# A two-layer streaming encoder on one core: halves of two attention output units moved into the end of attention, and the engines' loops written out

## What is computed

```python
for l in range(DEPTH):                                   # 2 layers
    h = rmsnorm(x, attn_norm_g[l])
    proj = h @ w_in[l]
    q, k, v, conv_in, gate_logits = jnp.split(proj, SPLITS, axis=-1)
    q, k = apply_rope(q), apply_rope(k)
    y_attn = sliding_window_sink_attention(q, k, v, attn_sinks[l]) @ w_attn_o[l]
    ca, cb = jnp.split(conv_in, 2, axis=-1)
    u = causal_dwconv(ca * sigmoid(cb), conv_dw_w[l], conv_dw_b[l])      # width 31
    y_conv = silu(layernorm(u, conv_ln_g[l], conv_ln_b[l])) @ w_conv_o[l]
    g_attn, g_conv = jnp.split(gate_logits, 2, axis=-1)
    x = x + (sigmoid(g_attn) * y_attn + sigmoid(g_conv) * y_conv) @ w_out[l]
    up = causal_dwconv(rmsnorm(x, ffn_norm_g[l]) @ w_ffn_up[l], ffn_dw_w[l], ffn_dw_b[l])   # width 3
    gt, val = jnp.split(up, 2, axis=-1)
    x = x + (silu(gt) * val) @ w_ffn_down[l]
return rmsnorm(x, final_norm_g)
```

## Time and profile before

| what | value |
|---|---|
| median of 3 runs | 914.47 us (913.42 to 919.29) |
| the profiled execution | 913.93 us |
| its span, first to last instruction | 912.1 us |
| mean granted TensorE clock | 0.976 |
| PE busy | 854.9 us, 94% |
| DVE, ACT, POOL busy | 620.8, 479.2, 406.5 us |
| read from HBM | 142.31 MB |

### The profile page before, as it was taken

How to read it: one execution, slowest core, us unless ns; L and a number is a source line. 1 busy time by engine, 2 the same in 40 slices (tenths; PEclk the granted TensorE clock), 3 DMA queues, 4 the chain that set the end, 5 groups by cost and what they waited for, 6 DMA issues and landing times.

```text
span 912.1 us, 18341 instructions
## 1 busy us (share of the span) xinstructions
PE 854.9 (94%) x6764; PEld 825.9 (91%) x6764; DVE 620.8 (68%) x1182; ACT 479.2 (53%) x714; POOL 406.5 (45%) x94
## 2 busy tenths in 40 slices
PE   2799999899999999999979999998999999999996
PEld 2799988788999999999969998896899999999995
DVE  6586889925368876656537878993535787566563
ACT  4354357636455655555555334774744656456455
POOL 4577735464722242232257873554574122422423
PEclk8899999999999999999989999999999999999998
DMA  7355423324444555455425552332434445545551
GB/s 263 114 180 177 177 93 139 139 93 140 155 153 155 185 192 195 168 193 181 176 96 185 186 185 93 140 139 93 139 139 152 172 181 188 187 181 184 184 184 47
DMA packets 20512, 144.20 MB, mean 158 GB/s; under 512 B 2400, under 2 KB 2656, under 8 KB 3296
## 3 DMA queue, kind: packets, MB, share of 16 engines
q1 hardware_dynamic: 19872, 142.62, 43.7%
q10 hardware_dynamic: 576, 0.75, 0.2%
HBM read 142.31 MB, written 1.05 MB: 157 GB/s over the span
## 4 chain that ended last, share of the span: by engine, by line
PE 71%; DVE 13%; issue 8%; ACT 5%; DMA 1%; ACTq 0%; DVEq 0%
PE pu L716 19%; PE pu L718 18%; PE pu L717 18%; DVE pc L492 4%; ACT whi L226 2%; PE ps L716 2%; PE ps L718 2%; PE ps L717 2%; DVE wlo L618 1%; PE pc L718 1%; PE pt L717 1%; PE pt L716 1%; PE pt L718 1%; PE pc L716 1%; PE po L737 1%
## 5 line engine op out<-in xcount | busy, mean ns | idle before, releaser
L198 POOL TENSOR_TENSOR wlo<-raw,whi 128x2048 fp32r<-128x2048 f32 x88 | 405.8, 4613 | 497.4 <-ACT whi L226 497.4
L226 ACT ACTIVATE whi<-raw 128x2048 fp32r<-128x2048 f32 x134 | 254.7, 1902 | 25.6 <-PE pu L718 22.7
L716 PE MATMUL pu<-hh,whi 128*128 128x256 f32 x800 | 233.4, 292 | 23.5 <-ACT hh L243 21.7
L716 PE MATMUL pu<-uh,whi 128*128 128x256 f32 x832 | 237.2, 285 | 5.4 <-DVE ul L596 3.2
L717 PE MATMUL pu<-ul,whi 128*128 128x256 f32 x832 | 235.4, 283 | 0.0
L718 PE MATMUL pu<-uh,wlo 128*128 128x256 f32 x832 | 235.4, 283 | 0.0
L718 PE MATMUL pu<-hh,wlo 128*128 128x256 f32 x800 | 228.2, 285 | 0.0
L717 PE MATMUL pu<-hl,whi 128*128 128x256 f32 x800 | 228.2, 285 | 0.0
L492 DVE SCALAR_TENSOR_TENSOR pc<-upad,par,pc 128x256 f32<-128x256 f32 x464 | 187.1, 484 | 0.3
L716 PEld LDWEIGHTS pu<-hh,whi 128*128 128x128 f32 x800 | 155.4, 194 | 27.5 <-ACT hh L243 22.5
L716 PEld LDWEIGHTS pu<-uh,whi 128*128 128x128 f32 x832 | 159.6, 192 | 7.8 <-issue 7.5
(11 more groups left out here) (142 smaller groups left out, 1144.7 us busy)
## 6 DMA issues: line engine op xcount, KB each, us to landing
raw<-in_weights SPq DMA_DIRECT2D x134, 1024.0 KB, 4.8
x<-in_x_t SPq DMA_DIRECT2D x2, 512.0 KB, 5.5
out_y<-qk SPq DMA_DIRECT2D x2, 512.0 KB, 2.6
par_all<-in_params ACTq DMA_DIRECT2D x1, 472.0 KB, 10.2
const<-in_const ACTq DMA_DIRECT2D x1, 130.0 KB, 7.0
probs<-in_positions ACTq DMA_DIRECT2D x1, 128.0 KB, 4.6
gf<-in_final_g ACTq DMA_DIRECT2D x1, 4.0 KB, 12.3
```

The source lines that it names most:

```text
L198: nc.gpsimd.tensor_tensor(wlo[s][:, :], raw[s][:, :], whi[s][:, :].bitcast(f32), ALU.subtract).then_inc(lo_ready[s], 1)
L226: A(whi[s][:, :], raw[s][:, :], ACT.Copy).then_inc(hi_ready[s], 1)
L716: MM(out, whi[s][:, w], hi, start=start, stop=False, skip_group_check=accumulate)
```

## The change

PE's end of attention: for the first two attention output units, the products with the first four channel tiles of o (the heads of the first key head, groups 0 to 3, complete since long) are split off as `group_half(i, 0)`: 24 matmuls each. Unit 21's stands before the last transposes, unit 22's between `values(6)` and `values(7)`. All of the first three mean pairs move behind `values(7)`, and the second halves follow them. ACT forms the high part of unit 23 before, and no longer behind, the last evictions.

All `Fori` loops become Python loops, so the counts waited for are constants; `par` becomes a slice of `par_all`, the copy goes, and `par_ready` counts 5 a layer and not 6. The sums of squares at the start no longer mark `unit_done`, so every count waited for on it is one less (`finished`). The two units beyond the last layer, their loads and splits, go.

```diff
+        def finished(l, u):
+
+            return uses(l, u) + 1
...
-            with sp.Fori(1, DEPTH * USES) as r:
+            for r in range(1, DEPTH * USES):
                 for s in range(RING):
                     sp.wait_ge(lo_ready[s], r)
-                    load_unit(s, bass.ds(r * RING + s, 1))
-
-            for s in range(AHEAD):
-                sp.wait_ge(lo_ready[s], DEPTH * USES)
-                load_unit(s, slice(DEPTH * UNITS + s, DEPTH * UNITS + s + 1))
+                    load_unit(s, slice(r * RING + s, r * RING + s + 1))
+
...
-                act.wait_ge(unit_done[s], l * USES + n + 1)
+                if l * USES + n > 0:
+                    act.wait_ge(unit_done[s], l * USES + n)
...
-            with act.Fori(0, DEPTH) as l:
+            for l in range(DEPTH):
+                par = par_all[:, l * NPAR:(l + 1) * NPAR]
...
                     A(gate[:, :, i, :], pu[u % RING][:, :, :], ACT.Tanh, scale=0.5).then_inc(gate_ready, 1)
-                    if i < NT - 1:
-                        next_high(l, u)
+                    next_high(l, u)
                 evict_transposed(GROUPS - 1)
                 high_of_o(GROUPS - 2)
                 high_of_o(GROUPS - 1)
-                next_high(l, U_AO - 1)
                 next_high(l, U_AO)
                 next_high(l, U_AO + 1)
...
-                V.tensor_copy(par[:, :], par_all[:, bass.ds(l * NPAR, NPAR)]).then_inc(par_ready, 1)
-                dve.wait_ge(par_ready, l * 6 + 1)
+            for l in range(DEPTH):
+
+                par = par_all[:, l * NPAR:(l + 1) * NPAR]
...
-                with dve.Fori(0, FFN_STEPS // 2 - 1) as r:
+                for r in range(FFN_STEPS // 2 - 1):
...
+                def group_half(i, group):
+
+                    s, n = (U_AO + i) % RING, uses(l, U_AO + i)
+                    if group == 0:
+                        pe.wait_ge(*result_read(l, U_AO + i - RING))
+                        pe.wait_ge(hi_ready[s], n + 1)
+                        pe.wait_ge(lo_ready[s], n + 1)
+                        pe.wait_ge(oh_ready, l * GROUPS + N_CHUNKS)
+                        pe.wait_ge(ol_ready, l * GROUPS + N_CHUNKS)
+                    else:
+                        pe.wait_ge(oh_ready, l * GROUPS + GROUPS)
+                        pe.wait_ge(ol_ready, l * GROUPS + GROUPS)
+                    for m in range(2):
+                        for k in range(GROUP_PAIRS * group, GROUP_PAIRS * (group + 1)):
+                            last = product(pu[s][:, m, :], s, 2 * k + m, oh[:, k, :], ol[:, k, :],
+                                           k == 0 and m == 0, k == NT - 1, True)
+                    if group == 1:
+                        last.then_inc(unit_done[s], 1)
+
                 for i in range(GROUPS):
                     if i + 1 < GROUPS:
                         standard(U_GATE + i + 1, hh, hl)
                     else:
-                        mean_pair(0)
-                        mean_pair(1)
+                        group_half(0, 0)
                     transpose_probs(i)
                     if i:
                         values(i - 1)
                     if i + 2 < GROUPS:
                         scores(i + 2)
-                mean_pair(2)
+                group_half(1, 0)
                 values(GROUPS - 1)
...
-                for i in range(2):
-                    standard(U_AO + i, oh, ol, o_ready if i == 0 else None)
+                for p in range(3):
+                    mean_pair(p)
+                group_half(0, 1)
+                group_half(1, 1)
                 mean_pair(3)
                 standard(U_AO + 2, oh, ol)
```

More of the change, by code:

```diff
@@ L87, in hybrid_encoder @@
         par_all = sb("par_all", [P, DEPTH * NPAR])
-        par = sb("par", [P, NPAR])
         gf = sb("gf", [P, NT])
@@ L260, in _ @@
                     u = U_GLU + i
-                    act.wait_ge(unit_done[u % RING], uses(l, u) + 2)
+                    act.wait_ge(unit_done[u % RING], finished(l, u))
                     if i >= 2:
@@ L371, in hidden_tile @@
                     for half, col in ((0, gcol), (1, vcol)):
-                        A(fbuf[:, ab, half, :], up[:, ab, half, :], ACT.Identity, scale=par[:, bass.ds(col + 2, 1)],
-                          bias=par[:, bass.ds(col + 3, 1)]).then_inc(f_conv0, 1)
+                        A(fbuf[:, ab, half, :], up[:, ab, half, :], ACT.Identity, scale=par[:, col + 2:col + 2 + 1],
+                          bias=par[:, col + 3:col + 3 + 1]).then_inc(f_conv0, 1)
                     if split is not None:
@@ L405, in _ @@
                 ffn_step(FFN_STEPS - 1, 0, True)
-                for s in range(AHEAD):
-                    split_high(l, s, USES)
+                if l < DEPTH - 1:
+                    for s in range(AHEAD):
+                        split_high(l, s, USES)
                 for i in range(4):
@@ L656, in hidden_tile @@
                         acc = fbuf[:, ab, half, shift:T]
-                        last = V.scalar_tensor_tensor(acc, up[:, ab, half, 0:T - shift], par[:, bass.ds(col, 1)], acc,
+                        last = V.scalar_tensor_tensor(acc, up[:, ab, half, 0:T - shift], par[:, col:col + 1], acc,
                                                       ALU.mult, ALU.add).then_inc(f_tap, 1)
@@ L744, in _ @@
             for p in range(NT // 2):
-                last = sum_pair(po[:, 0, :], sq, p, sq_ready, p + 1)
-                if p < RING:
-                    last.then_inc(unit_done[p], 1)
+                sum_pair(po[:, 0, :], sq, p, sq_ready, p + 1)
             pe.wait_ge(c_in, 16)
             swap, ident = const[:, C_SWAP:C_SWAP + P], const[:, C_ID:C_ID + P]
-            with pe.Fori(0, DEPTH) as l:
+            for l in range(DEPTH):
                 def standard(u, hi, lo, ready=None, between=None):
@@ L890, in ffn_step @@
                     down_unit(1, k - 2, 1 - parity)
-                with pe.Fori(0, FFN_STEPS // 2) as r:
+                for r in range(FFN_STEPS // 2):
                     ffn_step(r * 2 + 1, 1)
@@ L926 @@
     layers = []
-    units = np.zeros((DEPTH * UNITS + AHEAD, P, UNIT), np.float32)
+    units = np.zeros((DEPTH * UNITS, P, UNIT), np.float32)
     for l in range(DEPTH):
```

41 lines of the change are left out of this document (19 added, 22 removed).

## The result

| | kernel before | changed kernel |
|---|---|---|
| median | 916.88 us (913.42 to 919.63, 4 runs) | 905.93 us (904.79 to 906.86, 4 runs) |
| the profiled execution | 913.93 us, span 912.1 | 904.79 us, span 903.0 |
| mean granted clock | 0.976 | 0.985 |

The ratio of the two is 0.9884, with a 95% interval of 0.9855 to 0.9913: the change makes the kernel faster by 0.9 to 1.5%. Forecast were 907.5 us as the median and 907.1 for a profiled execution; measured were 905.93 and 904.79. The kernel before was 914.47 us when the forecast was made, the median of three runs, and is 916.88 with the fourth: its runs lie near 914 and near 919. So between the medians it is 10.95 us, or 1.16%, and between the profiled executions 9.14.

A forecast was written before the change was run, and what follows sets the result against it. TensorE, busy 94% of the span, was taken as the bound, so only its standing time could be won. 3.9 + 0.65 + 1.32 + 0.9 = 6.8 us off 913.93 gave 907.1 profiled, 907.5 median; range 903.5 to 911.5.

The forecast's parts named there:

- 1. Attention's end: From values(6) to mean_pair(3): 12.76 us of work at full clock, 14.67 expected; gain 2.1 and 1.8, together 3.9 us.
- the early split on ACT: High part of unit 23 formed ahead of ACT's last eviction: costs nothing, bound 0 to 1.9 us.
- the clock: Behind values(6) at attention's end: 4.3 us at the lower level taken, a loss of 1.9 us.
- S cannot move: S, the start of values(6) at 181.18 in layer 0, stays because PE waits there for DVE's low part of group 5.
- 2. The heads of the layers: Written-out loops at layer starts: 0.65 us in layer 0 and 1.32 at the boundary.
- The boundary: Between layers, DVE's small steps run while ACT works on the root: gain 1.32 us, bounds 0 and 1.32.
- 3. The head of the feed-forward loop: Without register work, 0.29 and 0.15 us less on two passes: 0.44 a layer, 0.9 in all, bounds 0 and 2.3.
- 4. At nothing: Register operations elsewhere, SP's static addresses, loads and splits beyond the last layer, dropped unit_done marks: no gain.
- The clock stays up: Rival: no lower clock at attention's end, gain 10.7 us, time 903.8; chance 0.12.
- The clock takes most of it: Rival: clock low for 6.8 us at attention's end, tail gives 1.7, sum 4.6, time 909.9; chance 0.18.
- Instruction supply: Rival: written-out code stalls on instruction fetches of 5.05 us each; four give 927.7 us; chance 0.05.
- The written-out part gives nothing: Rival: boundary bound by ACT's root in another way, attention's end alone gives 3.9, time 910.5; chance 0.07.

The follow-up runs named there:

- after: The changed kernel itself, its first runs and profile, against the kernel before: median 905.93 us, ratio 0.9884.
- tail_only: The kernel before with all its hardware loops, only the end of attention reordered on PE and ACT: 908.29 us, ratio to before 0.9914.
- late_split: The changed kernel with ACT's high part of unit 23 behind the last evictions again: 905.16 us, ratio to before 0.9881.
- loops_only: The changed kernel with the old end of attention on PE and ACT, loops still written out: 915.22 us, ratio to before 0.9983.
- loops_again: loops_only unchanged, for a second profile: 913.76 us.
- second_hole: The changed kernel with two mean pairs ahead of the last transposes again, unit 21's first half after values(6), unit 22's after the third mean pair: 910.63 us.
- fill: The changed kernel with both first-group halves ahead of values(6) and the mean pairs spread into remaining waits: 899.59 us, ratio to before 0.9818.
- after_again: The changed kernel unchanged, run again beside tail_only and loops_only: 906.78 us, ratio to before 0.9897.
- fill_dve: fill_hw with VectorE's loops alone written out, its parameter copy kept: 899.47 us, ratio to before 0.9821.
- fill_hw: The order of fill with the kernel before's hardware loops on every engine: 902.02 us, ratio to before 0.9845.

## Why the prediction was right, and where its steps missed

**The time and the sign** came out: 905.93 against 907.5 forecast, inside the range. The profiled gain was 9.1 against 6.8, 2.3 more. Part of that closeness is luck. The end of attention gave 2.55 us more than forecast and the row of taps 1.26 where nothing was forecast; the heads of the feed-forward loop, the start and layer 0's first units gave 1.5 less. And the median of before moved by 2.4 us with one more run: counted from 916.88, the forecast gain of 7.0 would have read 909.9. The measured 1.16% is over the 1% to which the prediction gave a chance of 0.18, but the interval, 0.9 to 1.5%, reaches to both sides of it.

**1. Attention's end.** The count of work was right within 0.1: 12.76 us forecast at the full clock, 12.67 and 12.68 measured wherever the clock was full (`after`, `tail_only`, `late_split`). The holes went as said: none ahead of the output units, the early split on ACT costs nothing (`late_split`), no wait for unit 22. The term that was mis-sized is the clock: 4.3 us of the lower level in each layer were taken, from the stretches of before, and worth 1.9. There are profiles of eight ends in the new order (the changed kernel and its repeat, `tail_only`, `late_split`): five show one stretch of 3.41 or 3.42 us, three none, none more. A stretch costs 1.5 us, so on average 0.9 a layer. (The two profiles of the changed kernel have a mean granted clock of 0.985 and 0.983, six of its ten runs 0.979, so its usual execution may have more.) The price of 0.44 us for each us was right; the length was taken too long, because I held the two holes that stay (1.23 and 1.57 us) for as bad as the old pair (2.65 and 1.14) with a third behind it. The hole ahead of the transposes was also 1.23 and not 1.76, or 1.50 with the hardware loops (`tail_only`).

| end of attention | idle times of PE, us | time at the lower clock in each profile, us |
|---|---|---|
| before, layer 0 (2 profiles) | 2.65, 1.14, 1.03 | 6.83, 6.83 |
| before, layer 1 (2 profiles) | 1.39, 1.60, 1.04 | 3.42, 3.42 |
| `loops_only`, `loops_again` | about 2.36, 1.1 to 1.6, 1.03 | 10.24, 10.24, 6.82, 10.24 |
| `second_hole` | 2.36, 1.1 to 1.6 | 6.83, 6.82 |
| the new order (8 ends) | 1.2 to 1.5 (once 0.25), 1.6 | 3.41 or 3.42 five times, none three times |
| the order of `fill` (8 ends) | 0.3 to 0.6 | none |

In this table the ends with an idle time of over 2.3 us had 6.8 to 10.2 us at the lower level, those whose longest was about 1.6 us had 3.4 or none, and those of `fill`'s order none. It is no law: 2.36 us brought 10.24 three times out of six where 2.65 brought 6.83. In layer 1 of before the first hole is 1.39 and not 2.65 because PE comes to it 1.5 us late from a stretch at the lower clock at 584.62, and the end with 0.25 us (`after_again`, layer 0) likewise from one at 143.12; there 1.0 of the 1.5 us went into the hole, and `values(6)` came only 0.5 late.

"**S cannot move**" was wrong. I counted DVE's 61.28 busy us of 62.40 as work that the change leaves alone. Part of the distance between its instructions was register work: written out, the same 174 instructions take 0.47 us less a layer (`fill_dve`), and S moves with them. That gave 1.26 us in the two profiles, of which about 0.25 (0.75 - 0.51 between the layers) is the stretch at 584.62; `tail_only`, with the loops and without that stretch, has 65.79 in layer 1 where before has 66.02. The large "issue" share of the chain, 8%, was no measure of it: 0.21 us stood behind every tap, but nearly all of it under the tap before.

**2. The heads of the layers.** The boundary was right to 0.01 us (1.31 for 1.32), and for the reason given: the small steps run while ACT forms the root, and the scaling takes 3.06 us instead of 0.29 beside POOL's split, and still ends before the root. In layer 0 the gain was 0.35 and not 0.65. Timeline of DVE there, changed kernel:

```profile
24.13 0.42 DVE L438 SCALAR_TENSOR_TENSOR aabs<-ang 128x256 f32<-128x256 f32 x1
24.59 0.29 DVE L462 TENSOR_SCALAR par_all<-par_all 128x248 f32<-128x248 f32 x1
```

The scaling follows directly (before it started 0.67 behind the end of `aabs`), so 0.63 of the 0.65 are there; but `aabs` itself ended 0.28 us later than in the profile before, because the steps ahead of it did. And more than the 0.35 was lost again by 115 us, namely 0.43: the first units ran at the lower clock from 27.50 to 32.30 and not from 27.85 to 31.66, 1.0 us more of it. This term was inside the noise of two executions, which the sum did not say.

**3. The head of the feed-forward loop** gave 0.14 for 0.9. The holes in PE were 0.47 and 0.66 us in either layer; they are 0.38 and 0.59 in layer 0 and 0.76 and 0.58 in layer 1, where 0.1 to 0.4 were forecast. In `fill_dve`, where DVE's register work is gone and the other engines' is not, they are 0.67 and 0.74, longer than in `fill_hw` (0.47 and 0.66). So DVE's register work did not hold PE there; that it lay beside the work of DVE and ACT is my reading, and why the first hole of layer 1 grew stays open. This is the same mistake as with S, in the other direction: I priced register work by its own length and not by what it lay beside.

**4. At nothing**: right as far as the medians can tell. The last norm took 9.05 and 9.06 us, and with PE's, ACT's, POOL's and SP's loops written out as well the median is the same as with DVE's alone (899.59 and 899.47).

**The rivals.** "The clock stays up" was true for one layer of the profile and three of eight ends; it is most of why the time came out lower (2.55 us; S gave 1.26). "The clock takes most of it" did not come in the new order, but it is what `loops_only` shows in the old one. "Instruction supply": the longest piece of "issue" in the changed kernel's chain is 0.48 us, where the layer's branch had 5.05. The Trainium skill (Advanced Engine Details and Errata, ISA Cache) states a cache of two lines of 256 instructions, larger on TensorE. By that, longer straight code must be fetched as it goes, and the pages of the profiles agree that more is fetched, 1.04 MB for 0.83. It could have stalled; on this kernel the fetch cost nothing that can be seen, and the large pieces of issue at the layer boundary stand behind DVE's branch. The instruction queues' lines on the page (packets, MB, share of 16 engines), changed kernel:

```profile
q8 instruction: 54, 0.88, 0.4%
q14 instruction: 19, 0.16, 0.1%
```

and kernel before:

```profile
q8 instruction: 38, 0.62, 0.3%
q14 instruction: 26, 0.21, 0.1%
```

"The written-out part gives nothing" is refuted by `fill_dve`: 2.55 us.

## What to carry to other kernels

When work is moved into the holes of the engine that bounds, count the holes that stay: with 1.2 and 1.6 us left standing, five ends of eight had a stretch at the lower clock that cost 1.5 us behind it, and filling them (2.25 us shorter at the full clock in each layer's end) brought 6.3 to 7.2 us in all. Before a loop is written out, look for the one engine whose chain crosses the branch or runs without a pause; here VectorE's alone gave all 2.55 us that the medians show, where 64 us of the chain had been named "issue". Weigh such a part in an order where the clock stays up, or it can vanish: the same loops gave 2.55 us in `fill`'s order and in the old one 1.5, which cannot be told from nothing.

## What the runs showed of the hardware that was not expected

- The changed kernel fell to the lower clock at one end of attention in one profile and at both in the next; `tail_only` and `late_split`, with the same order on PE, had it at the first end alone and at the second alone. In the new order 12.67 us and 14.18 us are the two lengths of the same 93 matmuls.
- The lower clock also came outside the ends of attention, over a stretch in which PE was busy throughout. Shortly before, PE had stood 1.03 us ahead of one `values`. In the second profile of the changed kernel (that standing, then the window of the stretch):

```profile
140.70 0.65 PE L798 MATMUL po<-probsT,vwin 128*64 128x256 f32 x4 [1.03 <-DVE ol L555]
```

```profile
143.12:146.53 3.41, 3.41 (x18) 3.41 (x17) 3.38 (x11) 1.87 (x7) 2.23 (x1) 0.50 0.13 24
```

  Both profiles of the kernel before have one like it in layer 1 (584.62 in the first, behind 1.13 us of standing that ended at 582.28). Every profile has that standing of 1.0 to 1.1 us in both layers, and in 3 of 26 cases a stretch followed it; filling the end of attention does not touch these.
- A VectorE instruction that takes 0.29 us alone took 3.06 beside GpSimd's weight split at the layer boundary, and the parameter copy 3.17 instead of 0.41. The Trainium skill (SBUF — State Buffer, SBUF: two separate sides) says that a pair of ports is shared by these two engines and held by one for a whole instruction, while the other waits. The profile agrees: GpSimd's two splits lie over this time, until 458.91, and VectorE's step ends just after them, at 459.06. The runs show the times, not the port:

```profile
449.79 9.12 POOL L198 TENSOR_TENSOR wlo<-raw,whi 128x2048 fp32r<-128x2048 f32 x2 [12.10 <-ACT whi L228]
```
